# Attention of a two-block model on one Trainium2 core: masks added by TensorE, scores read from PSUM, attention results split at once, the output projection begun inside the last units

## What is computed

```python
def causal_attention_blocks(q, k, v):          # 8 MLA heads, queries in blocks of 128
    for i in range(S // Q_BLOCK):
        lo, hi = i * Q_BLOCK, (i + 1) * Q_BLOCK
        s = jnp.einsum('bhqd,bhkd->bhqk', q[:, :, lo:hi], k[:, :, :hi])
        mask = jnp.arange(hi)[None, :] <= jnp.arange(lo, hi)[:, None]
        p = jax.nn.softmax(jnp.where(mask, s, -jnp.inf), axis=-1)
        outs.append(jnp.einsum('bhqk,bhkd->bhqd', p, v[:, :, :hi]))
...
o = jnp.concatenate([o_mla, o_moba], axis=-1)  # 8 MLA and 8 MoBA heads of 64
return o @ w_o                                 # 1024 x 1024, added to x
```

## Time and profile before

| | us |
|---|---|
| median of 3 runs | 1527.29 (1523.75 to 1528.34) |
| profiled execution, device time | 1534.74 |
| its span, first to last instruction | 1532.9 |
| TensorE busy | 1454.8 (95%) |
| VectorE busy | 1146.8 (75%) |
| ScalarE busy | 778.7 (51%) |
| GpSimd busy | 357.5 (23%) |
| mean granted clock of TensorE | 0.982 |

### The profile page before, as it was taken

The page is one execution under the profiler, slowest core; times in us unless marked ns, Lnnn a source line. Parts: engine busy times, 40 slices in busy tenths (PEclk is TensorE's granted clock), DMA queues, the critical chain, the costliest instruction groups (busy, mean ns, idle before and its releaser), DMA issues.

```text
span 1532.9 us, 28887 instructions
## 1 busy us (share of the span) xinstructions
PE 1454.8 (95%) x11238; PEld 1337.7 (87%) x11238; DVE 1146.8 (75%) x2293; ACT 778.7 (51%) x1581; POOL 357.5 (23%) x406
## 2 busy tenths in 40 slices
PE   7889999998899999999899999899999999999998
PEld 5667997677879988888788999899999999999997
DVE  5676985486768879968562989766767688888886
ACT  5685885554255545566454120244344366656563
POOL 7610001000100000001000012499887422211220
PEclk9999999999999999999799999999999999999999
DMA  7205553453358979843244669989999989988993
GB/s 247 79 28 171 171 173 127 124 170 94 116 169 290 316 273 342 302 142 118 70 142 136 210 233 336 339 319 341 346 338 342 322 311 333 319 307 309 319 321 135
DMA packets 97701, 355.64 MB, mean 232 GB/s; under 512 B 10896, under 2 KB 10896, under 8 KB 97312
## 3 DMA queue, kind: packets, MB, share of 16 engines
q1 hardware_dynamic: 67824, 245.50, 47.0%
q0 software_dynamic: 21968, 81.04, 15.3%
q10 hardware_dynamic: 7776, 27.27, 5.0%
HBM read 352.71 MB, written 1.05 MB: 231 GB/s over the span
## 4 chain that ended last, share of the span: by engine, by line
PE 64%; DVE 20%; DMA 9%; ACT 4%; issue 3%; POOL 0%; ACTq 0%; SPq 0%; DVEq 0%
PE ps L572 63%; DMA arena<-in_peer_v 7%; DVE arena L1258 5%; DVE w_lo L1258 4%; DVE arena L1264 2%; ACT w_hi L2116 2%; ACT arena L2113 1%; DVE arena L1978 1%; DVE arena L1261 1%; DVE act_hi_lo L1258 1%; ACT arena L2116 1%; DMA arena<-in_u_rows,arena 1%; DMA arena<-in_w_in 1%; DVE arena L1834 0%; DVE arena L1832 0%
## 5 line engine op out<-in xcount | busy, mean ns | idle before, releaser
L1258 DVE TENSOR_TENSOR w_lo<-arena,w_hi 128x512 fp32r<-128x512 f32 x680 | 455.2, 687 | 212.6 <-ACT w_hi L2116 207.3
L2116 ACT ACTIVATE w_hi<-arena 128x512 fp32r<-128x512 f32 x680 | 418.7, 627 | 314.2 <-PE ps L572 242.3
L572 PE MATMUL ps<-act_hi_lo,w_hi 128*128 128x256 f32 (+1 forms) x2496 | 562.0, 316 | 9.2 <-DVE w_lo L1258 5.0
L572 PE MATMUL ps<-arena 128*128 128x184 f32 (+10 forms) x5254 | 517.9, 280 | 24.0 <-DVE arena L1261 8.0
L572 PEld LDWEIGHTS ps<-arena 128*128 128x128 f32 (+2 forms) x5254 | 482.1, 162 | 57.9 <-issue 29.6
L572 PE MATMUL ps<-act_hi_lo,w_lo 128*128 128x184 f32 (+1 forms) x1760 | 460.6, 262 | 0.0
L572 PEld LDWEIGHTS ps<-act_hi_lo,w_hi 128*128 128x128 f32 x2496 | 422.1, 191 | 17.7 <-ACT w_hi L2116 9.4
L572 PE MATMUL ps<-w_hi,act_hi_lo 128*128 128x512 f32 (+2 forms) x960 | 314.4, 399 | 25.7 <-ACT w_hi L2116 9.5
L572 PEld LDWEIGHTS ps<-act_hi_lo,w_lo 128*128 128x128 f32 x1760 | 337.2, 192 | 0.0
L572 PEld LDWEIGHTS ps<-w_hi,act_hi_lo 128*128 128x128 f32 x960 | 183.9, 193 | 74.9 <-issue 20.8
L1258 DVE TENSOR_TENSOR arena<-arena 128x512 f32<-128x512 f32 (+17 forms) x304 | 188.1, 625 | 74.4 <-ACT arena L2113 69.1
(11 more groups left out here) (98 smaller groups left out, 661.5 us busy)
## 6 DMA issues: line engine op xcount, KB each, us to landing
arena<-in_w_ff SPq DMA_DIRECT2D x128, 512.0 KB
arena<-in_peer_u SPq DMA_DIRECT2D x128, 512.0 KB
arena<-in_peer_v SPq DMA_DIRECT2D x128, 512.0 KB
arena<-in_w_ada ACTq DMA_DIRECT2D x48, 512.0 KB, 5.1
arena<-in_w_glu SPq DMA_DIRECT2D x16, 512.0 KB
arena<-in_peer_wq SPq DMA_DIRECT2D x16, 512.0 KB
arena<-in_w_in SPq DMA_DIRECT2D x12, 512.0 KB
arena<-in_w_conv SPq DMA_DIRECT2D x12, 512.0 KB
```

The source lines that it names most:

```text
L572: return e.matmul(o, l, r, start=start, stop=stop)
L1258: return e.tensor_tensor(o, a, b, op)
L2116: return e.activation(o, a, ACT.Copy)
```

## The change

The mask or bias is added to the scores by TensorE, as a matmul of the identity with the mask into the same place in PSUM. VectorE takes the maximum from PSUM, ScalarE's exponential reads PSUM and frees the bank. VectorE copies the transposed probabilities of even units, ScalarE those of odd ones. In `mixer0` a result is split at once: ScalarE copies its high part, VectorE subtracts the low part (stage 8, so there are nine stages). TensorE does six of the eight chunks of the first half of `w_o` behind steps 18 to 23, and the two cutting engines move along. Block 3 of `w_in` uses banks 0 and 1. A small exponential ahead of the last MLA heads moves the load of its table. GpSimd's loads wait for result 15.

```diff
--- before
+++ after
@@ -296,7 +296,7 @@
     in_w = (512, 512, 512, 416)
-    in_bank = (0, 2, 6, 6)
+    in_bank = (0, 2, 6, 0)
     cT = V(SC, 3, 256)
@@ -305,7 +305,6 @@
     qt1, kt1, qt2, kt2 = V(QT1, 8, 256), V(KT1, 8, 256), V(QT2, 8, 256), V(KT2, 8, 256)
-    oT = V(OO, 8, 256)
     ATT_ST = 24576
@@ -327,7 +326,7 @@
                     vv = [[proj[:, kb, 1440 + 64 * h:1504 + 64 * h] for kb in range(2)] for h in hs]
-                units0.append(unit(128 * (t + 1), hs, t, qt, kt, d, vv, oT[:, 4 * fam + hp, t * 128:(t + 1) * 128]))
+                units0.append(unit(128 * (t + 1), hs, t, qt, kt, d, vv, [x[:, 4 * fam + hp, t * 128:(t + 1) * 128] for x in (HH, HL)]))
@@ -366,7 +365,8 @@
     mla_moba, window_att = Attention(units0), Attention(units1)
-    N_STAGES = 8
+    N_STAGES = 9
+    N_DRAIN = 6
@@ -757,7 +757,12 @@
                 for h in range(2):
-                    ins = mm(pb(bk, 2, c["K"])[:, h, :], c["q"][h], c["k"][h], True, True)
+                    s = pb(bk, 2, c["K"])[:, h, :]
+                    mm(s, c["q"][h], c["k"][h], True, False)
+                    if c["bias"] is not None:
+                        ins = mm(s, ident, c["bias"][:, h, :], False, True)
+                    else:
+                        ins = mm(s[:, c["K"] - 128:c["K"]], ident, sm("cmask"), False, True)
                 ins.then_inc(*mm_done(name, "scores", u))
@@ -795,7 +800,7 @@
             run(moba)
-            run(steps)
+            return steps
@@ -1179,20 +1184,25 @@
         weave(lin_tok("w_in2", 512, (6, 7), in_ready, "in", 2), side)
-        weave(lin_tok("w_in3", 416, (6, 7), in_ready, "in", 3), side)
+        weave(lin_tok("w_in3", 416, (0, 1), in_ready, "in", 3), side)
         run(side)
-        mixer0()
+        steps = mixer0()
         def mixed0(k):
-            if k == 0:
-                e.wait_ge(*alo_cut["mixed0", 3])
+            e.wait_ge(*bank[4]["mixer0", 2 * k])
+            e.wait_ge(*bank[5]["mixer0", 2 * k + 1])
         def turn_half():
-            for _ in range(12):
+            for _ in range(4):
                 yield
             yield
-        mix_out("w_o", mixed0, ((0, 1), (2, 3)), turn_half())
+        first = lin_tok("w_o", 512, (0, 1), mixed0, "w_o", 0)
+        for n, _ in enumerate(steps):
+            if n >= mla_moba.n + N_STAGES - 1 - 8 - N_DRAIN:
+                next(first)
+        run(first)
+        weave(lin_tok("w_o", 512, (2, 3), mixed0, "w_o", 1), turn_half())
         turn_x(1, 1, lambda t: e.wait_ge(*bank[2 + t]["w_o", 1]))
@@ -1329,8 +1339,8 @@
-        def lin_tok(done=None):
-            for k in range(8):
+        def lin_tok(done=None, begun=0):
+            for k in range(begun, 8):
                 chunk()
@@ -1443,25 +1453,15 @@
         def attention(name, att):
-            def mask(u):
-                c = att.units[u]
-                K, bk = c["K"], u % 2
-                sv, sp, nm = att.s(u), pb(bk, 2, K), att.NM[:, u, :]
+            def most(u):
+                c, bk, nm = att.units[u], u % 2, att.NM[:, u, :]
                 e.wait_ge(*mm_done[name, "scores", u])
-                if u >= 5:
-                    e.wait_ge(*turned[name, u - 5])
-                if c["bias"] is not None:
-                    tt(sv, sp, c["bias"], ALU.add).then_inc(bank[bk].sem, 1)
-                elif K == 128:
-                    tt(sv, sp, B(sm("cmask").unsqueeze(1), [128, 2, 128]), ALU.add).then_inc(bank[bk].sem, 1)
+                reduce = e.tensor_reduce(nm, pb(bk, 2, c["K"]), AX.X, ALU.max, negate=True)
+                if c["sink"] is None:
+                    reduce.then_inc(*masked(name, u))
                 else:
-                    tt(sv[:, :, 128:256], sp[:, :, 128:256], B(sm("cmask").unsqueeze(1), [128, 2, 128]), ALU.add)
-                    e.tensor_copy(sv[:, :, 0:128], sp[:, :, 0:128]).then_inc(bank[bk].sem, 1)
-                e.wait_ge(*bank[bk][name, u])
-                if c["sink"] is None:
-                    e.tensor_reduce(nm, sv, AX.X, ALU.max, negate=True).then_inc(*masked(name, u))
-                else:
-                    e.tensor_reduce(nm, sv, AX.X, ALU.max, negate=True).then_inc(*masked(name, "max", u))
+                    reduce.then_inc(*masked(name, "max", u))
                     e.wait_ge(*masked[name, "max", u])
@@ -1469,8 +1469,10 @@
                 sv, dn = att.s(u), att.DN[:, u, :]
-                e.wait_ge(*exped[name, u])
-                if att.units[u]["sink"] is not None:
+                if att.units[u]["sink"] is None:
+                    e.wait_ge(*bank[u % 2][name, u])
+                else:
+                    e.wait_ge(*exped[name, u])
                     tt(dn, dn, att.SE[:, u, :], ALU.add).then_inc(*shared(name, "sum", u))
@@ -1478,7 +1480,21 @@
-            yield from att_steps(att, (1, mask), (3, norm))
+            def probs(u):
+                bk = 2 + u % 2
+                if u % 2 == 0:
+                    e.wait_ge(*turned[name, u])
+                    if u >= 3:
+                        e.wait_ge(*mm_done[name, "values", u - 3])
+                    e.tensor_copy(att.p(u), pb(bk, att.units[u]["K"] // 64, 128)).then_inc(bank[bk].sem, 1)
+            def low_result(u):
+                if name == "mixer0":
+                    hi, lo = att.units[u]["o"]
+                    e.wait_ge(*ahi_cut["mixed0", u])
+                    tt(lo, ps[4 + u % 2][:, 0:128], hi.bitcast(F32), ALU.subtract).then_inc(bank[4 + u % 2].sem, 1)
+            yield from att_steps(att, (1, most), (3, norm), (5, probs), (8, low_result))
@@ -1491,7 +1507,8 @@
-        def mix_out(name, banks, gate=None, side=iter(())):
+        def mix_out(name, banks, gate=None, side=iter(()), begun=0):
             for j in range(2):
@@ -1502,7 +1519,7 @@
                 else:
-                    weave(lin_tok(done), side)
+                    weave(lin_tok(done, begun if j == 0 else 0), side)
@@ -2016,10 +2033,10 @@
         run(side)
-        run(attention("mixer0", mla_moba))
-        for c in range(4):
-            low(HL[:, 2 * c:2 * c + 2, :], oT[:, 2 * c:2 * c + 2, :], HH[:, 2 * c:2 * c + 2, :], "mixed0", c)
-        mix_out("w_o", ((0, 1), (2, 3)))
+        for n, _ in enumerate(attention("mixer0", mla_moba)):
+            if n >= mla_moba.n + N_STAGES - 1 - N_DRAIN:
+                chunk()
+        mix_out("w_o", ((0, 1), (2, 3)), begun=N_DRAIN)
         ffn(0, s5_tables())
@@ -2298,6 +2315,7 @@
             heads_root(8, ("moba", 1, 1))
+            act(stat("exp table", 1), sm("ones")[:, 0:1], ACT.Exp)
             yield from heads_T(8, 96, 1, qt1, sm("gqmla", 96), "gqmla", "mla", "q", 1)
@@ -2307,25 +2325,32 @@
             def exps(u):
-                sv, nm = att.s(u), att.NM[:, u, :]
+                c, sv, nm, bk = att.units[u], att.s(u), att.NM[:, u, :], u % 2
                 e.wait_ge(*masked[name, u])
+                if u >= 5:
+                    e.wait_ge(*turned[name, u - 5])
                 for h in range(2):
-                    ins = act(sv[:, h, :], sv[:, h, :], ACT.Exp, bias=nm[:, h:h + 1], accum_out=att.DN[:, u, h:h + 1])
-                if att.units[u]["sink"] is not None:
-                    ins = act(att.SE[:, u, :], att.SE[:, u, :], ACT.Exp)
-                ins.then_inc(*exped(name, u))
+                    ins = act(sv[:, h, :], pb(bk, 2, c["K"])[:, h, :], ACT.Exp, bias=nm[:, h:h + 1],
+                              accum_out=att.DN[:, u, h:h + 1])
+                ins.then_inc(bank[bk].sem, 1)
+                if c["sink"] is not None:
+                    act(att.SE[:, u, :], att.SE[:, u, :], ACT.Exp).then_inc(*exped(name, u))
                 bk = 2 + u % 2
-                e.wait_ge(*turned[name, u])
-                if u >= 3:
-                    e.wait_ge(*mm_done[name, "values", u - 3])
-                copy(att.p(u), pb(bk, att.units[u]["K"] // 64, 128)).then_inc(bank[bk].sem, 1)
+                if u % 2 == 1:
+                    e.wait_ge(*turned[name, u])
+                    if u >= 3:
+                        e.wait_ge(*mm_done[name, "values", u - 3])
+                    copy(att.p(u), pb(bk, att.units[u]["K"] // 64, 128)).then_inc(bank[bk].sem, 1)
                 e.wait_ge(*mm_done[name, "values", u])
-                copy(att.units[u]["o"], ps[bk][:, 0:128]).then_inc(bank[bk].sem, 1)
+                if name == "mixer0":
+                    copy(att.units[u]["o"][0], ps[bk][:, 0:128]).then_inc(*ahi_cut("mixed0", u))
+                else:
+                    copy(att.units[u]["o"], ps[bk][:, 0:128]).then_inc(bank[bk].sem, 1)
@@ -2335,11 +2360,13 @@
             run(moba)
-            run(steps)
-        def mix_out(side=iter(()), left=0):
-            for n in range(16 - left):
+            for n, _ in enumerate(steps, 8):
+                if n >= mla_moba.n + N_STAGES - 1 - N_DRAIN:
+                    chunk()
+        def mix_out(side=iter(()), left=0, begun=0):
+            for n in range(begun, 16 - left):
                 chunk()
@@ -2434,7 +2461,8 @@
```

(11 more changed lines are left out.)

## The result

The changed kernel takes 1564.5 us (median of four runs, 1553.9 to 1568.8) against 1527.8 us before (four runs beside it, 1523.8 to 1529.1): 1.0235 times, with an interval of 1.018 to 1.029. The forecast was 1535.1, with a range up to 1543. The sign was right; the time lies 21.5 us above the range and 29 us above the forecast. The profiled execution took 1566.45 us (span 1564.6) against 1534.74 (1532.9). The four executions had mean granted clocks of 0.972, 0.972, 0.975 and, in the fastest (1553.9 us), 0.989.

A forecast was written before the change was run, and what follows sets the result against it. The prediction took TensorE, with 64% of the chain of waits and no slack in the two stages touched, as the bound. It added +4.4 us in mixer0 and +3.4 in the window to 1527.3, giving 1535.1 us, range 1529 to 1543.

The forecast's parts named there:

- step 4: mixer0 masks by TensorE: +0.44 us a unit, 17.6 us instead of 14.1 from unit 8 to unit 12's transposes.
- rival C: mixer0's first units: the clock falls to half in the ring, +7 us, 1542 us in all; chance 0.15.
- Step 1: Other banks for w_in3: TensorE's 3.79 us wait goes, scores of unit 0 start at 76.8 us, 1.5 us earlier.
- Step 2: Exponential's table load moved out of mixer0's first units: 1.28 us, without the extra drain of about 1.38 us.
- Step 3: Scores kept in PSUM until the exponential, mixer0's first eight steps: unit 8 at 102.1 us, 8.4 us late.
- the ring: mixer0's first steps: scores, transposes, ScalarE's copy and exponential wait in a circle, 3.1 or 3.35 us a step.
- Step 5: Results split at once, w_o begun in mixer0's last units: 3.73 us idle goes, first half ends at 135.4 against 130.5.
- Step 6: Window attention, bias through TensorE: 5.2 us more work less 1.8 us of waits, +3.4 us, bounds 0 and +5.2.
- The sum: Whole kernel: +4.4 us by the end of w_o's first half and +3.4 in the window, +7.8 us.
- The range: Whole kernel: 1529 to 1543 us, leaving out the far end of rival C.

The follow-up runs named there:

- e6: Changed kernel with TensorE making each group of MoBA transposes one step earlier, two in the first step; 1535.5 us, 1.005 times the kernel before.
- e7: Kernel before with one pause put in: five extra VectorE reduces of unit 9's scores before their bank is freed; 1535.3 us, 1.0045.
- e5: Changed kernel with masks and biases added by VectorE again, exponentials reading SBUF and ScalarE copying all probabilities; 1520.6 us, 0.997 times the kernel before.
- e10: e5 with results copied to SBUF as in the kernel before and split in four cuts of two tiles; 1518.3 us, 0.9945 times the kernel before.
- e1: Changed kernel with ScalarE making each MoBA copy one step later, behind the exponential; 1555.8 us, 1.0185 times the kernel before.
- e16: e6 with both score matmuls ahead of the two mask or bias matmuls in each unit of both attentions; 1531.8 us, 1.0017 times the kernel before.
- e3: Changed kernel without the mask matmuls of mixer0, a probe of time alone; 1550.5 us, 1.0156 times the kernel before.

## Why the prediction was wrong in size

The steps are the numbered parts of the prediction. Two of its terms failed: the price of the masks in step 4, and the clock, which steps 4 and 5 took as full and rival C priced at 7 us.

- **Step 1**: right. Unit 0 at 75.63 us, forecast 76.8; the other runs with this part and the table load had it at 74.55 to 77.36.
- **Step 2**: right, no load among the exponentials of the changed kernel. The extra 1.4 us of the drain did not show: in ScalarE's timeline the load of 1.28 us stands at 71.31 us, right behind the record before it, and the next starts at 72.60.
- **Step 3**: the ring was right, link by link at full clock (3.38 and 3.27 us against 3.35 and 3.1). Unit 8 came 29.7 us behind unit 0, not 25.3. The links in the middle were stretched by the half clock, to 4.60 and 5.73 us (87.36 to 91.96 to 97.69).
- **Step 4**: the failed term of the sum. "+0.44 us a unit" came from a row in which the mask's neighbours have the same tile shape. In MoBA units it is 1.03 us, so the stage from unit 8 to unit 12 takes 22.3 us at full clock (92.50 to 114.82 in e6), not 17.6: 4.7 us.
- **Rival C** was the right one, at a chance of 0.15, and was priced wrongly: "each step's TensorE part doubles, some 1.4 us more in five steps: +7". The step that failed is the silent assumption in steps 4 and 5 that the clock is full again as soon as TensorE has no pause. In the same stage it stood at half for its whole length: 38.9 us (105.33 to 144.25) against 22.3 in e6, 16.6 us. With step 4's 4.7 that is the 21.3 us missed there. The kernel before held a hint, which I read as the clock's general price for a pause: there it came back 4.8 us into `w_o`, but among 512-column matmuls. It held another that no row showed: behind the window attention, from 733.40 to 753.70 us, its clock was at 0.50 with TensorE busy for 18.02 of 20.30 us. The Trainium skill, TensorE: Matmul & The Clock Gate, "HAM oscillation", which the prediction weighed, says that waits between bursts can keep the engine at 1.2 GHz. The traces agree that a wait can bring the clock down, and show more: in e7 one wait was enough for 17 us.
- **Step 5**: right. No pause ahead of `w_o`, and its matmuls at the full clock; from unit 12's transposes to the end of its first half 16.9 us, forecast 15.7, the first 2.5 us of it still at half clock. e5 and e10 show what it is worth where VectorE keeps up.
- **Step 6**: +6.9 us, forecast +3.4 with a bound at +5.2. The 1.8 us of idle time did go; TensorE's work grew by 8.7 us, not by 5.2, for the same reason as in step 4.
- **The sum**: 30.7 us by the end of `w_o`'s first half and 6.9 in the window make 37.6; the span grew by 31.7. The mean clocks put the changed kernel at 88 us of half clock in all (2 x 0.028 x 1564.6) and before at 55 us (2 x 0.018 x 1532.9). Over 50 us of the former lie in `mixer0`, so elsewhere it had less than before, which gives some of the difference back. Counted by matmuls from the end of both traces, the changed kernel is 40.0 us behind at 905 us of the kernel before, 34.9 at 1010 and 31.7 at the end. The first of these two steps is the clock: from 980 to 1020 us the kernel before had 0.82 and 0.93, where the changed one had 1.00 and 0.91 (1000 to 1040 us). The second has full clock in both and stays open.
- **The range** stopped at 1543, at the far end of C. It should have held "the units run at half clock": 4.5 us a pair doubled is 18 us more over four pairs, 1553. That would still have been 11 us short, by the masks' price in both attentions and the half clock in the ring, which it leaves out.

What stays open: which pauses bring the clock down, and why it stays down in the MoBA units. 1.46 us in e1 and 1.81 in e7 did, 1.49 in before did not, and the wait of 1.9 us ahead of unit 0 did in two traces of nine; no run here varied the length of a pause, or the tiles behind it, alone. Nor is it known whether the fastest execution of the changed kernel, with a mean clock of 0.989, had the long stretch at all.

## What to carry to other kernels

A wait on TensorE isn't always paid with its own length: behind it the granted clock can stay at half to the end of a stage of small matmuls, as it did here in the units with 64-row score tiles. So read the granted clock stage by stage, and order the queues of the other engines such that no result is needed right behind the work that makes it (here, transposes one step ahead of their copy, two lines for 29 us). Work moved to TensorE costs columns and changes of the stationary tile's shape too: put matmuls of one shape together, and leave on VectorE what it hides. Take the parts of a change one at a time: here half of it (banks, the early `w_o`) was worth 0.5 to 0.8%, and hidden under the other half.

## What was not expected of the hardware

- The granted clock stayed at 1.2 GHz for 41.0 us in the changed kernel and 36.8 us in e1 while TensorE had no gap, and returned only among the last transposes of the stage. The same instructions, with no pause ahead of unit 8, ran 26 us at 2.4 GHz (e6). Among the MLA units it came back in the midst of small matmuls (95.6 us in the changed kernel, 81.0 in e16).
- The same wait of 1.9 us at the same place, ahead of unit 0, was followed by half clock in two traces (e3, e16) and not in seven.
- A change among stationary tiles of 64x128, 128x128 and 128x64 costs 0.2 us at full clock; between 96 and 128 rows nothing that the rows show.
- At half clock a pair of units took 1.8 times as long, not twice (6.50 us in e3 against 3.62 before, 9.99 in the changed kernel against 5.67 in e6).
- The exponential was a little faster with PSUM as its source than with SBUF: 0.46 us for 256 columns against 0.50.
